# Output projections of a token mixer in other PSUM banks, and an activation-table load behind the last weight split

## What is computed

```python
def token_mixer(h, ...):
    z = h @ w_in + b_in
    q, k, v, glu_a, glu_b, gate_a, gate_b = split(z)
    a = chunked_rel_attention(q, k, v, rel_bias) @ w_attn_o            # 512 -> 1024
    u = glu_a * sigmoid(glu_b)
    u = silu(layer_norm(causal_dwconv(u, w_dw, b_dw), g_ln, b_ln))
    cb = u @ w_conv_o + b_conv_o                                       # 512 -> 1024
    y = sigmoid(gate_a) * a + sigmoid(gate_b) * cb
    return y @ w_mix_o

def conv_ffn(h, ...):
    u = causal_dwconv(h @ w_up, w_dw, b_dw)                            # 1024 -> 2 * 2816
    val, gt = split(u)
    return (gelu(gt) * val) @ w_down                                   # 2816 -> 1024

x = x + gt_m * rms_norm(token_mixer(...), g_post_mix)
x = x + gt_f * rms_norm(conv_ffn(...), g_post_ffn)                     # the output
```

## Time and profile before

| | |
|---|---|
| median of three runs | 779.14 us |
| the profiled execution | 779.02 us, its span 777.2 us |
| PE busy | 750.9 us, 97% of the span |
| DVE, ACT, POOL busy | 574.4, 393.5, 26.2 us |
| mean granted TensorE clock | 0.995 |
| HBM read | 147.02 MB, 191 GB/s over the span |
| chain that ended last | PE 74%, DVE 14%, ACT 7%, issue 3% |

### The profile page before, as it was taken

One profiled execution on the slowest core, in us unless ns is written; L12 is line 12 of the kernel. 1 busy time (PEld: TensorE's weight loads), 2 busy tenths in 40 slices (PEclk: granted clock), 3 DMA queues, 4 the chain that ended last, 5 costly groups with the idle time before them and its releaser, 6 DMA issues.

```text
span 777.2 us, 13336 instructions
## 1 busy us (share of the span) xinstructions
PE 750.9 (97%) x5280; PEld 690.9 (89%) x5280; DVE 574.4 (74%) x964; ACT 393.5 (51%) x665; POOL 26.2 (3%) x31
## 2 busy tenths in 40 slices
PE   7999999889999999999999999998999999999996
PEld 7988999877999999999889887898889999999994
DVE  5858888677677677679587988866857767676766
ACT  5472323565634454344473544475546556555554
POOL 0040000100000000000003000000010000000000
PEclk9999999999999999999999999999999999999999
DMA  7844354453499887889525423355335654555531
GB/s 295 286 132 153 109 170 157 142 169 124 162 354 361 308 284 270 278 294 371 176 96 177 163 82 114 131 190 190 118 126 185 214 198 163 192 197 180 174 126 55
DMA packets 40526, 148.94 MB, mean 192 GB/s; under 512 B 4496, under 2 KB 4624, under 8 KB 40080
## 3 DMA queue, kind: packets, MB, share of 16 engines
q1 hardware_dynamic: 39600, 142.91, 53.2%
q10 hardware_dynamic: 864, 5.18, 1.7%
HBM read 147.02 MB, written 1.05 MB: 191 GB/s over the span
## 4 chain that ended last, share of the span: by engine, by line
PE 74%; DVE 14%; ACT 7%; issue 3%; POOL 1%; DMA 1%; DVEq 0%; SPq 0%; ACTq 0%
PE bank L1034 13%; PE bank L1037 13%; PE bank L1035 13%; PE bank L1092 6%; PE bank L1090 6%; PE bank L1093 5%; PE bank L1068 5%; PE bank L1217 4%; DVE wlo L1447 3%; DVE arena L1453 3%; PE bank L1081 3%; DVE XN L1453 2%; ACT arena L1995 2%; ACT whi L1995 2%; DVE arena L1447 2%
## 5 line engine op out<-in xcount | busy, mean ns | idle before, releaser
L1034 PE MATMUL bank<-hh,whi 128*128 128x256 f32 x1000 | 286.9, 287 | 0.2
L1035 PE MATMUL bank<-hl,whi 128*128 128x256 f32 x1000 | 283.4, 283 | 0.0
L1037 PE MATMUL bank<-hh,wlo 128*128 128x256 f32 x1000 | 283.3, 283 | 0.0
L1447 DVE TENSOR_TENSOR wlo<-raw,whi 128x1024 fp32r<-128x1024 f32 x202 | 242.4, 1231 | 29.4 <-ACT whi L1995 29.1
L1995 ACT ACTIVATE whi<-raw 128x1024 fp32r<-128x1024 f32 x202 | 202.3, 1046 | 28.9 <-DMA raw<-w_dram 19.1
L1034 PEld LDWEIGHTS bank<-hh,whi 128*128 128x128 f32 x1000 | 192.1, 192 | 4.3 <-issue 2.0
L1035 PEld LDWEIGHTS bank<-hl,whi 128*128 128x128 f32 x1000 | 192.2, 192 | 1.5
L1037 PEld LDWEIGHTS bank<-hh,wlo 128*128 128x128 f32 x1000 | 192.1, 192 | 0.0
L1453 DVE SCALAR_TENSOR_TENSOR arena<-bank,cols,arena 128x255 f32<-128x255 f32 (+3 forms) x138 | 58.9, 480 | 27.9 <-ACT arena L1995 26.2
L1995 ACT ACTIVATE arena<-bank 128x256 f32<-128x256 f32 (+2 forms) x65 | 26.8, 421 | 93.8 <-PE bank L1037 73.6
L1092 PE MATMUL bank<-wlo,fh 128*128 128x512 f32 x176 | 69.2, 393 | 1.4 <-DVE wlo L1447 1.4
(11 more groups left out here) (176 smaller groups left out, 895.9 us busy)
## 6 DMA issues: line engine op xcount, KB each, us to landing
raw<-w_dram SPq DMA_DIRECT2D x268, 512.0 KB, 4.8
arena<-rows_dram ACTq DMA_DIRECT2D x1, 1792.0 KB, 8.1
X<-x_dram SPq DMA_DIRECT2D x2, 512.0 KB, 4.4
arena<-rows_dram ACTq DMA_DIRECT2D x1, 1024.0 KB, 11.6
arena<-bias_dram ACTq DMA_DIRECT2D x1, 1024.0 KB, 14.9
out_dram<-X SPq DMA_DIRECT2D x4, 256.0 KB, 2.1
const<-const_dram ACTq DMA_DIRECT2D x1, 640.0 KB, 3.8
arena<-bias_dram ACTq DMA_DIRECT2D x1, 512.0 KB, 5.9
```

Of the source, the lines that this page charges most:

```text
L1034: e.matmul(o, a, hh[:, k, :], start=(k == 0), stop=False)
L1035: e.matmul(o, a, hl[:, k, :], start=False, stop=False)
L1037: ins = e.matmul(o, wlo[:, s, k * 128:k * 128 + 128], hh[:, k, :], start=False, stop=(k == 7))
L1447: return e.tensor_tensor(out, a, b, op)
```

## The change

```diff
     def last_four(norm, tag, name, ks, src, block):
         ids = [P.unit("m", name, k, lead=0) for k in ks]
         P.need(ids[3], lead=1)
+        if norm is None:
+            P.step("table")
...
             for k in downs(up, j):
                 moving(P.unit("m", down, k), f"d{n}", k, k == 0, False, src=f"f{n}")
-        if first:
-            P.step(first)
         last_four(norm_next, f"d{n}", down, range(FT - 4, FT), f"f{n}", block)
...
     for name, tag in (("w_attn_o_2", "ao"), ("w_conv_o_2", "co")):
         for u in range(4):
-            P.fill(f"{tag}{u}", (0, 1, 6, 7)[u])
+            P.fill(f"{tag}{u}", (6, 7, 0, 1)[u])
...
-    ffn(2, None, "w_up_2", "w_down_2", 3, None, out2_block, "table")
+    ffn(2, None, "w_up_2", "w_down_2", 3, None, out2_block, None)
```

## The result

The changed kernel takes 773.83 us (median of five runs, 773.29 to 775.15) against 779.14 us before. The ratio is 0.9944, with a 95% interval of 0.9928 to 0.9960. Run again beside the experiments (`c_after`) it took 773.51 us (773.25 to 773.84) against 779.05, a ratio of 0.9932 (0.9919 to 0.9945). The change makes the kernel about 5 us faster, 0.4 to 0.8%. The profiled execution took 773.29 us, its span 771.5 us (before: 779.02 and 777.2).

A forecast was written before the change was run, and what follows sets the result against it. PE was taken as the bound (74% of the chain that ended last), its gaps being time lost. Terms 2.43 + 1.60 = 4.03 and 1.51 sum to 5.54 us, from 779.02 to 773.5 us; range 771.9 to 775.7.

The forecast's parts named there:

- The wait at `ao1` was for bank 1: Output projections: `ao1` waited for ACT to empty bank 1; with bank 7 it starts 2.43 us earlier.
- What is late next: Behind `ao1`: no bank or weight late, DVE waits some 0.9 us for `co0`, everything moves by the whole 4.03 us.
- Edit 2: End of program: table load behind the last high half, which starts 1.51 us earlier; Square and stores move by 1.51.
- the room of the load: At the first Square, ACT is 0.57 us early, so the moved table load is still hidden.
- Rival 1: Moved table load not hidden: ACT runs empty before it, Square 0.71 us late, 774.2 us; 6%.
- The slow stretch, 1.60 us: Behind the wait at `ao1`: without the wait the clock stays up and 18 matmuls save 1.60 us.
- Rival 2: Slow stretch stays elsewhere after 540 us, or was absent in most timed runs before: 1.60 not won, 775.1 us; 7%.
- Rivals 3, 4 and 5: DVE and ACT bound projections, 774.5 to 777.5 (6%); bank not the cause, 777.5 (2%); clock falls behind short waits, 780.3 (1%).

The follow-up runs named there:

- c_after: The changed kernel run again, on the same chip as the kernels with its parts: 773.51 us.
- Edit 1 alone: The kernel before with only the output projections moved to banks 6, 7, 0, 1, table load left where it was: 775.00 us, ratio 0.9953.
- e6: The kernel before with 10 plain float32 matmuls on constants into free bank 7 ahead of `ao1`: 778.68 us, ratio 0.9994.
- e7: The kernel before with the wait at `ao1` filled by 19 matmuls of the projections' own form: 778.49 us, ratio 0.9996.
- e1: The kernel before with only the output projections in banks 6, 7, 0, 1, first five runs: 775.00 us, ratio 0.9953.
- e1b: The kernel before with only the output projections in banks 6, 7, 0, 1, run again later: 774.95 us.
- e6b: The kernel before with 10 plain float32 matmuls in the wait at `ao1`, repeated for another profile: 777.42 us.
- e6c: The kernel before with 10 plain float32 matmuls in the wait at `ao1`, repeated once more for a profile: 778.95 us.
- e3: The kernel before with 20 plain float32 matmuls into free bank 7 ahead of `ao1`, which started 2.0 us late: 779.69 us.
- e2: The kernel before with only the table load moved behind the last high half: 776.65 us, ratio 0.9977.
- e5: The changed kernel with the last high half made inside the last Gelu step: 773.03 us, ratio to the kernel before 0.9924.
- e8: The kernel before, banks unchanged, with 19 projection-form matmuls in the wait at `ao1` and the table load behind the last high half: 776.07 us.
- after: The changed kernel, both edits, in its first runs and profile: 773.83 us, profiled execution 773.29 us.

## Why the prediction was right

The forecast was 773.5 us and 5.54 us of gain; measured were 773.83 and 773.51, and 5.3 and 5.5 us by the medians. The idle time and the table load were right as mechanisms; that the 1.60 us of the clock came out as well is in part luck.

- *The wait at `ao1` was for bank 1.* Right. Edit 1 alone removed it, with 2.49 us between the lowest runs for a term of 2.43.
- *What is late next.* Right to 0.1 us at each step: DVE idle 0.21 us ahead of `ao(3)`, 0.99 ahead of `co0`, no bank and no weight late, everything behind it moved as a whole (219.03 and 219.01 us).
- *Edit 2.* Right: 1.50 for a term of 1.51, the room of the load 0.58 for 0.57. Rival 1 is refuted by two runs.
- *The slow stretch, 1.60 us.* Right for the profiled execution and for the medians, but the step behind it was too simple. I wrote that in this trace the clock fell only behind PE's two longest waits, and took the stretch at `ao1` as the price of the wait at `ao1`. The runs show that it falls at other places too, in other executions: near 164 us behind the wait of 2.0 us that I had held up as the one without a fall, and in the tail behind waits of 0.97 and 0.70. Where it does not fall at `ao1`, it may fall in the tail. So 1.60 is not saved by keeping PE at work at `ao1` (e6, e7: 0.3 us by the medians, ratios of 0.9994 and 0.9996, no difference that can be told). With the change it is saved by the medians: the gain is 5.54 us there and 3.91 by the lowest runs, 1.63 apart, and the changed kernel has neither the wait at `ao1` nor the two waits together in the tail. Which of the two matters how much is not shown, since edit 1 alone keeps the tail's waits and still gained its 4.05.
- *Rival 2* held a part of the truth: in 20 of 67 runs of the kernel before there was, by their times and mean clocks, no such stretch where it costs. Measured against those the change gains 3.9 us. The Trainium skill (TensorE: Matmul & The Clock Gate, "What's actually happening") calls the number of slow matmuls at a kernel's start run-variable; the stretches here lie far behind the start, and the groups show that they vary as well. Because the medians of before lie in the group with the stretch, the forecast held. One trace could not tell that, and the profiled execution happened to be of that group.
- *Rivals 3, 4 and 5* did not happen. Of the changed kernel's ten runs one is above the rest, 775.15 us, 1.3 us over the median of its five, with a mean clock of 0.994 against 0.996 to 0.998 of the others. It was not profiled, and the stretch near 164 us, which neither edit touches, is the one known that would fit.

Open: why edit 1 alone, whose tail has the same two waits, was in the lowest group in 10 of 11 runs, while the kernel with the wait filled was there in 3 of 12 (e7) and 5 of 11 (e6). Its tail comes 2.5 us earlier, and the rows point at that. Counted from the start of `ao0`, PE's matmul behind the tail's first wait starts at 236.7 us in e1 and e1b, at 239.2 in e6, e6b, e6c and e7, at 240.7 in the profile of before and at 241.1 in e3. Only at 239.2 does a fall follow, in two of four profiles; e3, whose wait at `ao1` is filled like theirs, has 8 of 11 runs in its lowest group. That is a correlation over eight profiles: a run that shifts the tail by steps, with all else left, would test it.

## What to carry to other kernels

An engine's wait for a bank can be the other engine's order and not its load: `gg7` was complete 4.3 us before ACT read it (its last matmul ends at 525.83, ACT reads from 530.10), and giving the next unit a bank that is long free cost nothing and took the wait off the path. A table load goes behind the last work that others wait for, as close ahead of its user as the idle time there allows, and that room can be measured by adding loads. And before a slow stretch of the clock is priced, look at several executions: groups of times a constant step apart are its sign, and closing one place may not take the group of slower times away (e6, e7).

## What was not expected of the hardware

- The clock fell to 0.50 in the tail behind two waits of 0.97 and 0.70 us with one matmul between them, though in the first profile the same waits were followed by 1.00. Near 164 us it fell in three of the fourteen profiles (e2, e5, e8) and not in the others.
- Slow stretches come together. Four profiles have none near 142 us (`after`, `e1b_banks`, `e6_busy10`, `e6b_busy10`), and these have none anywhere while PE works, from 11 us on. Every profile with one near 164 us, at `ao1` or in the tail has one near 142 us too. It is a difference between executions and not between kernels: `after` and `c_after` are the same kernel and differ in it, and so are `e6b_busy10` and `e6c_busy10`.
- What a slow stretch costs depends on its place. One near 142 us cost nothing that can be told (line 1317 at 171.84 to 172.65 in the seven profiles that have it and not the one near 164, 172.05 to 172.18 in the four that have neither), one near 164 from 1.4 to 1.8 us (173.53, 173.61 and 173.97, against a median of 172.1).
- A plain float32 matmul on 128 columns stands in the profile as two records 0.11 to 0.12 us apart (20 of them took 4.4 us), a float32r one on 256 columns as one record, 0.12 us behind the one before.
